# A two-layer streaming trunk on one core: pauses re-ordered, token numbers stored once, and the time-step row in two passes

## The chip, the core and the metric

The kernel runs as one program on one core of a Trainium2 chip. The metric is the time of one execution on the device, in microseconds (us). The engines are called by their names or by those of the profile: TensorE is PE (its weight loads are PEld), VectorE is DVE, ScalarE is ACT, GpSimd is POOL and SyncE is SP. SP issues nearly all DMA transfers.

## What is computed

The input is a sequence of 256 tokens of 1024 channels, in float32. It passes two layers. Each normalises its input, projects it for four token mixers (short gated convolution, state-space mixer, spatial gating, trailing pooling), merges their outputs by sigmoid gates and adds the projected result; then it normalises again and applies a feed-forward part, which is dense in layer 0 and picks 2 of 8 experts for each token in layer 1. A last norm ends it. Cut to what matters here:

```python
for layer in range(2):
    h = rmsnorm(x, norm1_g[layer])
    pa, pb, pc, pd = jnp.split(h @ w_in[layer], [...], -1)
    y_a = short_conv_mixer(...)
    z, xbc, dt_raw = jnp.split(pb, [...], -1)   # dt_raw: 16 heads
    y_b = mamba2_mixer(z, xbc, dt_raw, ...)     # ends with a norm over 4 groups
    y_c, y_d = gmlp_mixer(...), pool_mixer(...)
    gates = sigmoid(h @ w_gate[layer])          # (tokens, 4, 1024)
    merged = sum(gates[:, :, i] * (y @ w_br[layer]) for i, y in enumerate((y_a, y_b, y_c, y_d)))
    x = x + merged @ w_out[layer]
    h2 = rmsnorm(x, norm2_g[layer])
    x = x + (swiglu(h2, ...) if layer == 0 else moe_ffn(h2, ...))   # top 2 of 8 experts
return rmsnorm(x, final_g)

def moe_ffn(x, router_w, wg, wu, wd):
    ...
    for e in range(8):
        out = out + combine[:, e:e + 1] * swiglu(xt, wg[e], wu[e], wd[e])
```

## The kernel before

**Products.** A float32 product of full precision is made from rounded parts. Activations and weights are each split into a high part, rounded to TensorE's faster float32 format, and a low part, the rest. A product is then three matmuls: high by high, high by low and low by high (`product`, L1453). Some small products are made with plain float32 operands; the profile counts each of those as two instructions. `mm` (L1445) issues every matmul, so nearly all of TensorE's time stands on that line.

**Weights.** All weights come as units of 128 x 2048 float32 values (1 MB). SP loads them into a ring of `RING` = 3 slots (7 in the expert stage). ScalarE rounds a unit to its high part (`split`, L416; `split_e`, L448), VectorE subtracts to get the low part (L745, L789), and TensorE uses the unit and raises `unit_used`, which frees the slot. Both engines split `AHEAD` = 2 units ahead of TensorE. A layer's mixers have 54 units: 0 to 23 the input projection, 24 to 41 the gates and output projections of three branches, 42 to 45 the gate of the state-space branch, 46 to 49 its projection, 50 to 53 the output projection. The dense feed-forward has 33 units (11 steps of 3). An expert item has 42 units, in 7 chunks of 6.

**Order.** The engines run their own instruction streams and meet at semaphores. The order of the mixers' smaller work around the units is a list written by hand, `PLAN` (L69): pairs of a stage's name and the number of units that follow. Every engine walks this list. On ScalarE the convolutions, `var`, `spatial`, `pool_out` and `short` are run behind the split of the unit that follows them; every other stage, and on VectorE all of them, is run ahead of it.

**The norms** (`norm_sums`, L1479). ScalarE squares the pairs of channel tiles (L433). GpSimd adds the second and the third pair to the first (`squares_added`, L1326). TensorE sums over the channels with a matrix of ones: four products, of tiles 0, 1, 6 and 7. This is called three times: for the dense part's norm in layer 0, and for layer 1's two norms. The dense part's input rows are `yb_hi`/`yb_lo`, the mixers' are `h_hi`/`h_lo`.

**The time steps.** The weights of the 16 time-step columns are split on their own into `wdt_hi` and `wdt_lo`. TensorE makes a row of 16 x 256 with 24 matmuls (stage `dt_row`), ScalarE copies it, and TensorE transposes it in two halves (stage `dt_in`).

**State-space norm** (stage `y_norm`, the last of `PLAN`). TensorE spreads the groups' sums over the channels, VectorE multiplies by them (L1021) and makes the low part (L748), ScalarE the high part of `yb`. Unit 46 is the first to use them. Stage `short` (L538 on ScalarE) makes the short convolution's rows `y_hi`/`y_lo` in the same way, and `pool_out` those of the pooling.

**Experts.** After the router, every expert's tokens are packed into items of up to 128 rows; with these inputs there are 8 items. Seven of them run in a loop (`body`), the last behind it. An item's units are the gate, up and down weights, chunk by chunk. The rows of a coming item are gathered from DRAM (`rows`) by GpSimd with an indirect DMA, whose row numbers are made thus: VectorE compares the slots with a counting row (`picks`, L1155), TensorE multiplies the result by the token numbers behind chunk 3 (four instructions), and VectorE copies the column to integers (`row_id`). Ahead of the loop, TensorE makes the first item's hidden rows from units 0 to 3 (`up`, L1791), then uses unit 4 and turns the hidden rows for the way down (L1892); VectorE splits units 4, 5 and 6, multiplies the gate (`gated`, L1179) and splits unit 7.

**The end.** The last item's results go to DRAM (`made`), come back in each token's order and are added; the final norm follows. ScalarE scales the rows of one half of the tokens by the norm, VectorE those of the other; each half of the tokens is stored by one transfer.

## Time and profile before

| | |
|---|---|
| time, median of 3 executions | 1858.77 us (1858.38 to 1862.35) |
| the profiled execution | 1860.32 us |
| its span | 1858.5 us |
| TensorE's mean granted clock | 0.997 of full speed |
| TensorE busy | 1838.1 us, 99% of the span, 10331 matmuls |
| VectorE, ScalarE, GpSimd busy | 80%, 64%, 10% |
| DMA, mean over the span | 280 GB/s |

The span runs from the first to the last instruction that the profiler recorded; the rest of an execution's time lies around it. The times of the rows further down are counted from the span's start. A matmul's recorded duration is longer than the distance to the next one, since matmuls are pipelined: those of 512 columns last 0.39 us and start 0.227 apart, those of 256 columns last 0.28 and start 0.12 apart.

### The profile page before, as it was taken

What the parts mean: (1) busy time and instruction counts of PE and PEld (TensorE: products, weight loads), DVE (VectorE), ACT (ScalarE), POOL (GpSimd) and SP (SyncE); (2) the same over time, 40 slices, a digit from 0 to 9 for tenths busy, and PEclk for the clock granted to TensorE, in tenths of its full rate; (3) what the DMA queues carried; (4) which work ended last, traced back from release to release, by engine and by line L of the source; (5) the groups of instructions that cost most, each with busy time, mean ns of one, the idle gap of its engine ahead of it and who ended that gap; (6) DMA issues with size and microseconds to landing.
All of it is one profiled execution on the core that took longest, in us unless ns stands there. A gap on an engine that the chain in (4) does not pass through costs nothing.

```text
span 1858.5 us, 27339 instructions
## 1 busy us (share of the span) xinstructions
PE 1838.1 (99%) x10331; PEld 1595.2 (86%) x10331; DVE 1483.2 (80%) x1308; ACT 1192.8 (64%) x1010; POOL 193.7 (10%) x147
## 2 busy tenths in 40 slices
PE   9999999999999999999999999999999999999997
PEld 8998878999999998779788888888888888888876
DVE  7776677755578866776988988888899898988887
ACT  5655654533346546555767777777777777877775
POOL 1055000000010460000840000000000000000010
PEclk9999999999999999999999999999999999999999
DMA  9454455455454444446799999999999999999994
GB/s 355 173 182 159 160 180 176 165 184 188 174 200 164 154 179 169 172 160 237 303 375 372 385 389 377 367 373 393 384 377 375 369 394 378 373 375 381 385 393 174
DMA packets 74545, 521.27 MB, mean 280 GB/s; under 512 B 8176, under 2 KB 8432, under 8 KB 13680
## 3 DMA queue, kind: packets, MB, share of 16 engines
q1 hardware_dynamic: 71568, 509.34, 72.7%
q0 software_dynamic: 2912, 11.01, 1.6%
q8 instruction: 47, 0.77, 0.2%
q14 instruction: 18, 0.15, 0.0%
HBM read 509.83 MB, written 10.49 MB: 280 GB/s over the span
## 4 chain that ended last, share of the span: by engine, by line
PE 94%; DVE 2%; DMA 2%; ACT 1%; issue 1%; SPq 0%; DVEq 0%; ACTq 0%
PE psum L1445 92%; PE psum L1892 1%; DMA weight_raw<-mix_w 1%; DMA weight_raw<-moe_w 1%; DVE proj L1021 0%; PE psum L1820 0%; DVE yb_lo L748 0%; DVE weight_raw_r L789 0%; DVE yb_lo L755 0%; PE psum L1528 0%; PE psum L1652 0%; DVE proj L771 0%; DVE weight_lo L1035 0%; DVE weight_lo L745 0%; ACT proj L717 0%
## 5 line engine op out<-in xcount | busy, mean ns | idle before, releaser
L745 DVE TENSOR_TENSOR weight_lo<-weight_raw,weight_hi 128x2048 fp32r<-128x2048 f32 x139 | 329.3, 2370 | 151.8 <-ACT weight_hi L416 150.8
L416 ACT ACTIVATE weight_hi<-weight_raw 128x2048 fp32r<-128x2048 f32 x139 | 265.2, 1910 | 144.2 <-PE psum L1445 140.4
L1445 PE MATMUL psum<-weight_lo,y_hi 128*128 128x512 f32 x768 | 304.3, 396 | 0.0
L1445 PE MATMUL psum<-weight_hi,y_hi 128*128 128x512 f32 x768 | 301.2, 392 | 2.4 <-DVE y_lo L748 1.8
L1445 PE MATMUL psum<-weight_hi,y_lo 128*128 128x512 f32 x768 | 299.8, 390 | 0.0
L1445 PE MATMUL psum<-weight_lo,y_lo 128*128 128x512 f32 x672 | 262.5, 391 | 0.0
L1445 PE MATMUL psum<-weight_raw_r,y_hi 128*128 128x512 f32 x576 | 224.9, 390 | 0.0
L1445 PE MATMUL psum<-proj_r,y_hi 128*128 128x512 f32 x576 | 224.4, 390 | 0.0
L1445 PE MATMUL psum<-h_hi,weight_hi 128*128 128x256 f32 x704 | 201.1, 286 | 0.0
L1445 PE MATMUL psum<-h_lo,weight_hi 128*128 128x256 f32 x704 | 199.2, 283 | 0.0
L1445 PE MATMUL psum<-h_hi,weight_lo 128*128 128x256 f32 x704 | 199.2, 283 | 0.0
L789 DVE TENSOR_TENSOR weight_raw_r<-weight_raw,weight_lo 128x2048 fp32r<-128x2048 f32 x72 | 165.0, 2291 | 36.6 <-ACT weight_lo L448 36.1
L789 DVE TENSOR_TENSOR weight_raw_r<-weight_raw,weight_hi 128x2048 fp32r<-128x2048 f32 x72 | 166.1, 2307 | 25.1 <-ACT weight_hi L448 24.6
L448 ACT ACTIVATE weight_hi<-weight_raw 128x2048 fp32r<-128x2048 f32 x72 | 138.2, 1919 | 64.7 <-DMA weight_raw<-moe_w 63.4
L789 DVE TENSOR_TENSOR proj_r<-proj,weight_hi 128x2048 fp32r<-128x2048 f32 x72 | 164.7, 2288 | 13.0 <-ACT weight_hi L448 13.0
L789 DVE TENSOR_TENSOR proj_r<-proj,weight_lo 128x2048 fp32r<-128x2048 f32 x72 | 164.9, 2291 | 11.1 <-ACT weight_lo L448 10.4
L1445 PEld LDWEIGHTS psum<-weight_hi,y_hi 128*128 128x128 f32 x768 | 144.3, 188 | 33.3 <-DVE h_hi L789 2.0
L1445 PEld LDWEIGHTS psum<-weight_hi,y_lo 128*128 128x128 f32 x768 | 144.4, 188 | 30.3
L448 ACT ACTIVATE weight_lo<-weight_raw 128x2048 fp32r<-128x2048 f32 x72 | 138.1, 1919 | 49.8 <-DMA weight_raw<-moe_w 49.6
L1445 PEld LDWEIGHTS psum<-weight_lo,y_hi 128*128 128x128 f32 x768 | 144.5, 188 | 28.5
L448 ACT ACTIVATE weight_hi<-proj 128x2048 fp32r<-128x2048 f32 x72 | 138.6, 1925 | 36.2 <-DMA proj<-moe_w 31.2
L448 ACT ACTIVATE weight_lo<-proj 128x2048 fp32r<-128x2048 f32 x72 | 138.3, 1921 | 27.4 <-DMA proj<-moe_w 26.5
(315 smaller groups left out, 3802.0 us busy)
## 6 DMA issues: line engine op xcount, KB each, us to landing
proj<-moe_w SPq DMA_DIRECT2D x144, 1024.0 KB, 6.9
weight_raw<-moe_w SPq DMA_DIRECT2D x144, 1024.0 KB, 6.8
weight_raw<-mix_w SPq DMA_DIRECT2D x106, 1024.0 KB, 4.8
first_raw<-moe_w SPq DMA_DIRECT2D x48, 1024.0 KB, 7.0
weight_raw<-ff_w SPq DMA_DIRECT2D x33, 1024.0 KB, 4.8
made_rows<-zeros POOLq DMA_DIRECT2D x1, 4096.0 KB, 22.1
made_rows<-pool_tmp SPq DMA_DIRECT2D x8, 512.0 KB, 6.4
weight_raw<-mix_w SPq DMA_DIRECT2D x4, 512.0 KB, 8.4
```

The costliest lines, as they stand in the source:

```text
L416: A(hi[:, slot, :], raw[:, slot, :], ACT.Copy).then_inc(hi_done, 1)
L448: A(hi_e(v), raw_e(v), ACT.Copy).then_inc(hi_done, 1)
L745: V.tensor_tensor(lo[:, slot, :], raw[:, slot, :], hi[:, slot, :].bitcast(f32), ALU.subtract).then_inc(lo_done, 1)
L789: V.tensor_tensor(lo_e(v), raw_e(v), hi_e(v).bitcast(f32), ALU.subtract).then_inc(lo_done, 1)
L1445: return nc.tensor.matmul(o, a, b_, start=start, stop=stop, skip_group_check=True, **k)
L1892: last = nc.tensor.transpose(bank(6)[:, f * P:(f + 1) * P], ff_h[:, f * P:(f + 1) * P], C_("ident"))
```

## The change

- **Norm sums.** GpSimd adds all four pairs of squares into the first and then the two tiles of that pair; TensorE makes one product where it made four.
- **Time-step row.** `wdt_hi` and `wdt_lo` stand side by side in one tile of 32 columns. 16 matmuls replace 24; the row has 32 partitions, and two plain float32 products with `both` (two identity matrices, one over the other) add its halves and turn it.
- **Order of stages.** `y_norm` is run behind the split of the unit that follows, on ScalarE and VectorE; VectorE also runs `short` and the pooling's low part (`pool_low`) so.
- **End of the dense layer.** On VectorE the low part of pair 2 goes ahead of the addition of pair 3.
- **Token numbers.** GpSimd writes the token of every packed row into a DRAM tensor `ids` with four indirect transfers, once. In the loop it loads 128 numbers per item from there. The picks on VectorE, the product on TensorE and the copy of its result go away in the loop; GpSimd waits for `gather_ps` where it waited for `id_done`.
- **First expert units.** `first_up` begins each of the first two units with the products that don't need the rows' low part. VectorE multiplies the first gate ahead of the split of unit 6.
- **Start and end.** SP loads the first half of x ahead of the parameters. The last scaling and the stores are cut in halves of 512 channels.

```diff
+        wdt = sb("wdt", [P, KT, 2 * HEADS], f32r)
+        wdt_hi, wdt_lo = wdt[:, :, 0:HEADS], wdt[:, :, HEADS:]
+        both = sb("both", [2 * HEADS, HEADS])
...
@@ sync
-            sp.dma_start(par[:, :PAR_FIRST], par_in[0, :, :PAR_FIRST]).then_inc(par_loaded, 16)
             for u in range(2):
                 for part in range(2):
                     if u == 0:
                         sp.dma_start(x[:, 4 * part:4 * part + 4, :], x_in[:, 4 * part:4 * part + 4, :]).then_inc(x_loaded[part], 16)
+                    if u == part == 0:
+                        sp.dma_start(par[:, :PAR_FIRST], par_in[0, :, :PAR_FIRST]).then_inc(par_loaded, 16)
...
-            for t in range(TT):
-                sp.wait_ge(*((S["tok_std"], 2 * TT + 1), (S["rstd_done"], 3))[t])
-                sp.dma_start(out[:, t, :], x_gain[:, t, :]).then_inc(stored, 16)
+            for n in range(2):
+                for t in range(TT):
+                    sp.wait_ge(*((S["tok_std"], 2 * TT + 1 + n), (S["rstd_done"], 3 + n))[t])
+                    sp.dma_start(out[:, t, cols(n)], x_gain[:, t, cols(n)]).then_inc(stored, 16)
@@ scalar
-                    behind = name.startswith("conv") or name in ("var", "spatial", "pool_out", "short")
+                    behind = name.startswith("conv") or name in ("var", "spatial", "pool_out", "short", "y_norm")
...
-                for u in range(u, MIX_UNITS):
-                    mixer_unit(layer, u)
+                for m in range(u, MIX_UNITS):
+                    mixer_unit(layer, m, "y_norm" if m == u else None)
@@ vector
                 for name, n in PLAN:
-                    stage(name, layer)
-                    for _ in range(n):
-                        mixer_unit(layer, u)
+                    behind = {"pool_out": "pool_low", "short": "short"}.get(name)
+                    if behind != name and name != "y_norm":
+                        stage(name, layer)
+                    for m in range(n):
+                        mixer_unit(layer, u, behind if m == 0 else None)
                         u += 1
-                for u in range(u, MIX_UNITS):
-                    mixer_unit(layer, u)
+                for m in range(u, MIX_UNITS):
+                    mixer_unit(layer, m, "y_norm" if m == u else None)
...
+                        if q == PAIRS - 1:
+                            low(2, q - 1)
                         added(q)
-                        if q:
+                        if 0 < q < PAIRS - 1:
                             low(2, q - 1)
...
-                    if c == 3 and not final:
-
-                        dve.wait_ge(S["id_ps"], item + 1)
-                        V.tensor_copy(row_id, bank(7)[:, SEQ:SEQ + 1]).then_inc(S["id_done"], 1)
...
-            for v in (4, 5, 6):
-                split_e(v)
+            split_e(4)
+            split_e(5)
             dve.wait_ge(unit_used, RING + MOE_U + 4)
             gated(0, 0)
+            split_e(6)
             split_e(7)
@@ gpsimd
-                for q in (1, 2):
+                for q in range(1, PAIRS):
                     gp.wait_ge(S["sq_done"], PAIRS * n + q + 1)
-                    last = G.tensor_tensor(flat(sq[:, 0:2, :]), flat(sq[:, 0:2, :]), flat(sq[:, 2 * q:2 * q + 2, :]), ALU.add)
-                    if q == 1:
-                        link(last)
-                last.then_inc(S["sq_added"], 1)
+                    link(G.tensor_tensor(flat(sq[:, 0:2, :]), flat(sq[:, 0:2, :]), flat(sq[:, 2 * q:2 * q + 2, :]), ALU.add))
+                G.tensor_tensor(sq[:, 0, :], sq[:, 0, :], sq[:, 1, :], ALU.add).then_inc(S["sq_added"], 1)
...
+            G.tensor_copy(at_id, made_f).then_inc(S["ids_at"], 1)
+            gp.wait_ge(S["ids_at"], 1)
+            gp.wait_ge(made_cleared, 32)
+            for n in range(2):
+                for t in range(TT):
+                    at_ = bass.IndirectOffsetOnAxis(ap=at_id[:, TT * n + t:TT * n + t + 1].bitcast(u32), axis=0)
+                    gp.indirect_dma_start(ids, at_, tok_id[:, t:t + 1], None).then_inc(ids_landed, 16)
...
             with gp.Fori(0, last_item) as item:
-                gp.wait_ge(S["id_done"], item + 1)
+                gp.wait_ge(S["gather_ps"], 2 * item + 2)
+                gp.dma_start(row_id, ids[ds((item + 2) * P, P), :]).then_inc(ids_landed, 16)
+                gp.wait_ge(ids_landed, 16 * (item + 1 + 2 * TT))
@@ tensor
-                for k in (0, 1, KT - 2, KT - 1):
-                    if k == 0:
-                        pe.wait_ge(S["sq_added"], n + 1)
-                    elif k == KT - 2:
-                        pe.wait_ge(S["sq_done"], PAIRS * (n + 1))
-                    last = mm(bank(7)[:, 0:SEQ], C_("ones"), sq[:, k, :], k == 0, k == KT - 1)
-                last.then_inc(S["norm_sum"], 1)
+                pe.wait_ge(S["sq_added"], n + 1)
+                mm(bank(7)[:, 0:SEQ], C_("ones"), sq[:, 0, :], True, True).then_inc(S["norm_sum"], 1)
...
-                        mm(o, wdt_hi[:, k, :], h_hi[:, k, :], k == 0, False)
-                        mm(o, wdt_hi[:, k, :], h_lo[:, k, :], False, False)
-                        last = mm(o, wdt_lo[:, k, :], h_hi[:, k, :], False, k == KT - 1)
+                        mm(o, wdt[:, k, :], h_hi[:, k, :], k == 0, False)
+                        last = mm(o, wdt[:, k, :], h_lo[:, k, :], False, k == KT - 1)
...
-                        last = nc.tensor.transpose(bank(6)[:, SEQ + t * HEADS:SEQ + (t + 1) * HEADS], row[:, t * P:(t + 1) * P],
-                                                   C_("ident")[0:HEADS, 0:HEADS])
+                        last = mm(bank(6)[:, SEQ + t * HEADS:SEQ + (t + 1) * HEADS], row[:, t * P:(t + 1) * P], both[:], True, True)
...
+            def first_up(half):
+
+                split_e_is(half, 0)
+                pe.wait_ge(S["eg_hi_done"], half + 1)
+                for k in range(4):
+                    w, kk = slice(k * CHUNK_F, (k + 1) * CHUNK_F), 4 * half + k
+                    mm(bank(4), xg_hi[:, kk, :], hi_e(half)[:, w], kk == 0, False)
+                    mm(bank(4), xg_hi[:, kk, :], lo_e(half)[:, w], False, False)
+                pe.wait_ge(S["eg_lo_done"], half + 1)
+                for k in range(4):
+                    kk = 4 * half + k
+                    last = mm(bank(4), xg_lo[:, kk, :], hi_e(half)[:, k * CHUNK_F:(k + 1) * CHUNK_F], False, kk == KT - 1)
+                last.then_inc(unit_used, 1)
...
-                    if c == 3 and not final:
-
-                        pe.wait_ge(S["pick_done"], item + 2)
-                        for t in range(TT):
-                            last = mm(bank(7)[:, SEQ:SEQ + 1], pick[:, t, :].bitcast(f32), C_("tok_id", t, 1), t == 0, t == 1)
-                        last.then_inc(S["id_ps"], 1)
...
-            for v in range(4):
-                if v < 2:
-                    pe.wait_ge(S["eg_lo_done"], v + 1)
-                if v == 2:
-                    pe.wait_ge(S["x_tok_done"], 2 * TT)
-                up(bank(4 + v // 2), v, v % 2)
+            first_up(0)
+            first_up(1)
+            pe.wait_ge(S["x_tok_done"], 2 * TT)
+            up(bank(5), 2, 0)
+            up(bank(5), 3, 1)
```

## Rows read from the trace of the kernel before

**Rows 1.** The page, busy time and share of the span of each engine.

```profile
PE 1838.1 (99%) x10331; PEld 1595.2 (86%) x10331; DVE 1483.2 (80%) x1308; ACT 1192.8 (64%) x1010; POOL 193.7 (10%) x147
```

**Rows 2.** Timeline of TensorE, dense layer: start us, us, engine, line, what.

```profile
351.80 1.89 PE L1445 MATMUL psum<-proj,con 128*128 128x256 f32 x8
...
353.34 0.47 PE L1445 MATMUL psum<-yb_hi,weight_hi 128*128 128x256 f32 x1
```

**Rows 3.** Timelines of ScalarE, VectorE and GpSimd, start and end of the dense layer.

```profile
348.07 0.62 ACT L433 ACTIVATE proj<-x 128x512 f32<-128x512 f32 x1
...
351.17 2.28 DVE L745 TENSOR_TENSOR weight_lo<-weight_raw,weight_hi 128x2048 fp32r<-128x2048 f32 x1
...
537.39 2.86 POOL L1330 TENSOR_TENSOR proj<-proj 128x512 f32<-128x512 f32 x2 [191.45 <-ACT proj L433]
```

**Rows 4.** Timelines of TensorE and VectorE, time-step row of both layers.

```profile
36.08 0.28 PE L1445 MATMUL psum<-h_hi,wdt_hi 128*16 128x256 f32 x1 [0.90 <-DVE h_lo L748]
...
562.22 1.48 DVE L748 TENSOR_TENSOR h_lo<-proj,h_hi 128x512 fp32r<-128x512 f32 x2
...
564.58 0.28 PE L1445 MATMUL psum<-h_hi,wdt_hi 128*16 128x256 f32 x1
...
567.39 0.28 PE L1445 MATMUL psum<-h_hi,weight_hi 128*128 128x256 f32 x1
```

**Rows 5.** Chain that ended last, two stretches of one item: start us, us, work.

```profile
1057.39 16.37 PE psum L1445 x72
...
1074.20 16.88 PE psum L1445 x76
```

**Rows 6.** Timelines of TensorE and VectorE, start of the experts.

```profile
898.82 0.48 PE L1445 MATMUL psum<-weight_hi,y_hi 128*128 128x512 f32 x1
...
903.80 0.44 PE L1892 MATMUL psum<-con,proj 128*128 128x128 f32 x2 [1.98 <-DVE proj L1179]
...
895.21 3.54 DVE L789 TENSOR_TENSOR weight_raw_r<-weight_raw,weight_hi 128x2048 fp32r<-128x2048 f32 x1
...
900.87 2.28 DVE L789 TENSOR_TENSOR h_hi<-first_raw,weight_hi 128x2048 fp32r<-128x2048 f32 x1
...
903.07 0.67 DVE L1179 TENSOR_TENSOR proj<-proj,psum 128x512 f32<-128x512 f32 x1
...
910.28 0.68 DVE L748 TENSOR_TENSOR y_lo<-psum,y_hi 128x512 fp32r<-128x512 f32 x1
```

**Rows 7.** Timelines of TensorE and VectorE, end of the dense layer.

```profile
541.18 0.38 PE L1445 MATMUL psum<-yb_hi,weight_hi 128*128 128x256 f32 x1 [1.04 <-DVE yb_lo L755]
...
542.25 2.55 DVE L745 TENSOR_TENSOR weight_lo<-weight_raw,weight_hi 128x2048 fp32r<-128x2048 f32 x1
```

**Rows 8.** Timelines of TensorE and VectorE, SSM norm of layer 0.

```profile
291.51 0.40 PE L1445 MATMUL psum<-weight_hi,h_lo 128*128 128x512 f32 x1
...
293.66 3.22 DVE L1021 SCALAR_TENSOR_TENSOR proj<-proj,par,psum 128x256 f32<-128x256 f32 x8 [2.71 <-PE psum L1445]
...
296.81 2.43 DVE L748 TENSOR_TENSOR yb_lo<-proj,yb_hi 128x1024 fp32r<-128x1024 f32 x2
...
299.39 0.47 PE L1445 MATMUL psum<-weight_hi,yb_hi 128*128 128x512 f32 x1 [0.28 <-DVE yb_lo L748]
```

**Rows 9.** Timelines of ScalarE and TensorE, short convolution of layer 0.

```profile
168.13 1.92 ACT L416 ACTIVATE weight_hi<-weight_raw 128x2048 fp32r<-128x2048 f32 x1 [4.12 <-PE psum L1445]
...
173.31 0.39 PE L1445 MATMUL psum<-weight_hi,y_hi 128*128 128x512 f32 x1
```

**Rows 10.** Stretches: us, busy us (count) by engine, TensorE clock, DMA share, GB/s.

```profile
903.80:907.20 3.40, 3.40 (x17) 2.89 (x18) 3.40 (x2) 2.41 (x2) 3.40 (x2) 1.00 1.01 423
...
1797.20:1800.60 3.40, 1.61 (x9) 1.17 (x8) 3.40 (x3) 2.90 (x2) 0.00 (x0) 1.00 1.02 424
...
1800.60:1804.00 3.40, 3.40 (x10) 2.63 (x9) 3.40 (x3) 2.38 (x2) 0.00 (x0) 0.50 1.00 417
```

**Rows 11.** Timeline of ScalarE, last scaling.

```profile
1852.96 1.15 ACT L727 ACTIVATE proj<-proj,small 128x1024 f32<-128x1024 f32 x1 [0.23 <-DVE small L1309]
```

59 lines of the change are left out of this document (31 added, 28 removed).

## The prediction

> **What bounds the kernel now.** I began with the busy line [rows 1]: TensorE is busy for 1838.1 of 1858.5 us. The other engines have slack, so an edit counts only if it takes instructions off TensorE, or shortens or lengthens one of its few pauses. The longest wait of TensorE is 2.0 us [rows 6], so I read the timelines around each pause and asked of every moved step: when does TensorE need its result, and when will it have it now?
>
> **Terms that take work off TensorE.**
>
> *Norm sums.* Each of three calls issues four products, recorded as eight instructions, from 351.80 to the next matmul at 353.34 [rows 2]: 1.54 us. One product is a quarter, so each call sheds about 1.2 us. In exchange GpSimd adds the last pair of squares and folds the pair, and TensorE waits for that.
> In the dense layer the last squares end at 348.07 + 0.62 = 348.69 [rows 3]. A GpSimd addition of 512 columns takes 1.43 (two in 2.86 [rows 3]), and one of 256 columns half of it. That makes 350.8, or 351.2 with two semaphores, before 351.80. The saving stands: -1.2. If the fold has to stand behind VectorE's next split (351.17, 2.28 us [rows 3]), it ends near 354.2 and the term turns to about +1.2.
> The Trainium skill has a rule here (SBUF — State Buffer, section "SBUF: two separate sides"): VectorE with two SBUF inputs and a GpSimd operation that reads SBUF take an exclusive lock, and the later one waits for the whole instruction. By that rule the fold is either in time or a whole split late, and nothing between.
> In layer 0, TensorE stands before the time-step row until 36.08, waiting 0.90 for h_lo [rows 4], which in the code stands behind ACT's and VectorE's splits of the first weight units, not behind the sums alone. The time saved only lengthens this wait: 0. Putting x ahead of the parameters moves the same bytes ahead of those weights: 0 too.
> In layer 1, the two last pairs of h_lo are finished at 562.22 + 1.48 = 563.70 and TensorE wants them at 564.58 [rows 4]. This chain starts at TensorE's unit before, not at the sums, so only the slack of about 0.8 can be had: -0.8 (from 0 to -1.2).
>
> *Time-step row.* 24 matmuls run from 564.58 to 567.39 [rows 4], 0.117 us each; 8 fewer in each layer is -1.9. The two transposes that follow become plain f32 products, which this kernel records as two instructions each. The nearest price is four such small instructions in 0.51 us [rows 5]: two more per layer, about +0.25, together +0.5 (between 0, if only the streaming counts, and 0.5).
>
> *Token numbers.* Seven of the eight items carry a stretch of 76 matmuls in 16.88 us where the others have 72 in 16.37 [rows 5]. The difference, 0.51 us, is the product with the token numbers, now taken out: 7 x 0.51 = -3.6. 72 matmuls of the stretch take 72 x 0.227 = 16.4, so there is no pause in it that could take this back. GpSimd instead writes the numbers once with four small indirect transfers and reads 128 of them per item before its gather. It waits on its own queue alone, an item ahead of need. I take 0; it would cost only if the rows came later than five such stretches on, 5 x 16.4 = 82 us.
>
> **Terms on pauses.**
>
> *Start of the experts.* The new order lets TensorE start its first expert unit without the low part, under 1 us earlier. But unit 4 then waits: its split runs from 895.21 for 3.54 us, to 898.75, and TensorE uses it at 898.82 already [rows 6]. This half is 0. The second half is real. TensorE stands until 903.80 for the product that VectorE makes at 903.07, behind the split that began at 900.87. With that split moved behind, the product starts at 900.87 and ends at 901.55; TensorE has issued unit 4 at 901.65 (12 matmuls of 0.23 after 898.82), so 2.1 us go. What is late next: VectorE works without a break from 895.21 to 910.96, where the low part of the hidden rows ends [rows 6]. TensorE, 2.1 earlier, would now want it about 0.6 before it is there. Net -1.5 (from -2.1 to -0.8).
>
> *End of the dense layer.* The low part of pair 2 goes ahead of the addition of pair 3. TensorE gets pair 2 at 541.18 [rows 7]; the first of its two instructions still ends with GpSimd's additions at 537.39 + 2.86 = 540.25 [rows 3], so it gains 0.2. But the addition of pair 3 slips by 1.8, and ACT and the low part of pair 3 with it; the weight split queued behind them slips from 542.25 to about 543.4 [rows 7]. TensorE needs this split 36 matmuls of 0.12 us after pair 2, at 545.3. It ends at 545.7, or, if GpSimd's new third addition (1.4 us, woken near 543.1) comes between, at 547.0. So +0.4 or +1.7 (from 0 to 1.7): I take +1.0.
>
> *The SSM norm moves behind a split.* This is the largest term, and it is a loss. VectorE has stood for 2.71 us when the spread sums come at 293.66; then it normalises and makes both low parts, until 299.24. TensorE starts on them at 299.39, after a pause of 0.28 [rows 8]. Now the split of unit 47 comes first. It can't fill the idle 2.71: its high part goes into a slot that is free only when unit 44 is used, and TensorE's last matmul of that unit ends at 291.51 + 0.40 = 291.91 [rows 8]. ACT needs 1.92 [rows 9], so VectorE could split from 293.95 to 296.2 at the earliest. The norm then starts 2.5 later and TensorE with it, in both layers: 2 x 2.5 = +5.1. The bounds are 0 (split hidden) and 2 x 2.9.
>
> *The short convolution's low part moves behind a split.* ACT finishes the high part of that split at 168.13 + 1.92 = 170.05. VectorE then splits to 172.3 and makes the low part (1.21, half of two in 2.43 [rows 8]) to 173.5, and TensorE wants it at 173.31 [rows 9]. With a restart +0.4 per layer, +0.8 (from 0 to 1.2). The pool's low part moves behind a split in the same way, but several units ahead of its first use: 0.
>
> *Output in halves.* The last scaling takes 1.15 [rows 11]. Its halves let stores start about 0.5 earlier, and the fourth store costs one more issue. I take -0.3 (from 0 to -0.6).
>
> **Sum.** -1.2 - 0.8 - 1.9 + 0.5 - 3.6 - 1.5 + 1.0 + 5.1 + 0.8 - 0.3 = -1.9 us.
>
> **The clock.** Near the end TensorE paused and was busy for 1.61 of 3.40 us; in the next 3.40 its granted clock was 0.50, that is 1.2 instead of 2.4 GHz [rows 10]. Half speed for 3.40 us costs at most 1.7; I take 1.6. The pause of 1.98 before 903.80 [rows 6] drew none: 1.00 in the 3.40 us behind it [rows 10]. The new pause before the SSM product is 0.28 + 2.5 = 2.8, twice: I expect a spell after one of the two, +1.6, which makes -0.3.
>
> The Trainium skill speaks against this change here (TensorE: Matmul & The Clock Gate, section "HAM oscillation — how this bites in real kernels"): where the engine waits for its input between bursts, each wait can throttle it and the next burst starts at the low clock. By that rule both pauses draw a spell and the sum would be +1.3; the trace agrees with its one spell and disagrees with its 1.98 us pause.
>
> The profiled execution took 1860.3 us, 1.8 of it around its span of 1858.5, and is 1.5 over the median of 1858.8. The sum is made against that span; the 1.8 around it stay, so the difference is carried over to the median: 1858.8 - 0.3 = **1858.5**.
>
> **Rivals.**
> - *Forecast* (0.45): both y_norm pauses grow, with one or two slow spells: -0.3 to +1.3, 1858.5 to 1860.1.
> - *No spell* (0.17): the pause before 903.80 speaks for it. -1.9, 1856.9.
> - *The split hides* (0.15): the norm is not late, because VectorE gets the high part before its idle 2.7 us. Against it: ACT can't write the slot before unit 44 is used. -1.9 - 5.1 = -7.0, 1851.8.
> - *The item time does not fall* (0.08): if the arrival of weights held the loop, the 3.6 would be lost: +1.7, 1860.5 with no spell, 1862.1 with one. Against it: a stretch is as long as its matmuls make it [rows 5].
> - *Slower* (0.15): the clock, after the two long pauses, stays at half for most of the unit that follows. At half clock each us costs 0.5, so it decides once the two spells together last more than 2 x (3.7 + 1.9) = 11.2 us; at 6.6 us each they cost 6.6 and it is -1.9 + 6.6 = +4.7, 1863.5. Against it: the one spell seen had ended after 3.4 us with TensorE busy.
>
> **Numbers.** 0.2% is 3.7 us, about what a measurement here can tell. Faster: the hidden split 0.15 and 0.05 for other terms better than taken. Slower: 0.15 plus 0.02 of the fourth case with two spells. Same: the rest, 0.63. The range goes from 1853.0 to 1863.0; outside lie the third case and part of the last, together about 0.2. The terms' own bounds (-0.8 to +0.6 at the experts and the dense layer's end, 2.4 at the fold) fit in it.
>
> **What will show it.** In the profile after: TensorE before its first product with yb_hi waits about 2.8 us for VectorE's yb_lo in both layers, with the granted clock at 0.50 behind at least one; before the first product with y_hi and the short convolution's rows a new wait of 0.3; the norm sums x2 instead of x8; the wait at the expert start gone from 2.0 to nearly 0, with a new short one for y_lo some 7 us on; the stretches of 76 matmuls gone from the seven items, each item 0.5 shorter. The prediction is wrong if yb_lo is not late, if the fold misses its moment, or if an item does not shorten.

## The result, and the profile after

The changed kernel takes 1866.85 us (median of 6, 1863.32 to 1868.91) beside 1859.37 for the kernel before (6, 1858.36 to 1862.35). The ratio is 1.0038, with a 95% interval of 1.0028 to 1.0048: about 7 us slower. The prediction was 1858.5 with a range up to 1863.0. The time lies above the range, in the case "slower", which had been given 0.17.

The profiled execution of the changed kernel took 1865.16 us, with a span of 1863.2; that is 4.7 over the span of before. The page and the waits of TensorE show the kind of thing that happened:

```profile
PE 1832.1 (98%) x10273; PEld 1588.1 (85%) x10273; DVE 1472.8 (79%) x1289; ACT 1188.8 (64%) x1011; POOL 247.2 (13%) x167
```

```profile
PE psum L1458 <- DVE yb_lo L754: 5.5, 2, 2.8
PE psum L1458 <- DVE y_lo L754: 4.3, 3, 2.7
PE psum L1458 <- POOL proj L1334: 2.1, 1, 2.1
PE psum L1458 <- DVE h_lo L754: 2.1, 2, 1.7
...
PE psum L1458 <- DVE weight_lo L751: 1.2, 1, 1.2
PE psum L1458 <- DVE weight_raw_r L795: 1.1, 2, 0.6
```

(Columns: who waited for whom, us in total, times, the longest.) TensorE is busy for 6.0 us less than in [rows 1], so the work did leave it. It stands longer: for yb_lo as forecast; for two things that the sum did not hold, a GpSimd addition (L1334, the fold) and y_lo 2.7 us long; and for a weight split (L751), which the sum held in its +1.0 for the end of the dense layer.

The reader can place each gain and loss by comparing the start of one and the same instruction of TensorE in both traces. The rows of after that answer to those of before:

```profile
36.45 0.28 PE L1458 MATMUL psum<-h_hi,wdt 128*32 128x256 f32 x1 [1.69 <-DVE h_lo L754]
...
173.39 0.47 PE L1458 MATMUL psum<-weight_hi,y_hi 128*128 128x512 f32 x1
...
302.05 0.47 PE L1458 MATMUL psum<-weight_hi,yb_hi 128*128 128x512 f32 x1 [2.75 <-DVE yb_lo L754]
...
356.75 0.70 PE L1458 MATMUL psum<-proj,con 128*128 128x256 f32 x2 [2.11 <-POOL proj L1334]
357.10 0.47 PE L1458 MATMUL psum<-yb_hi,weight_hi 128*128 128x256 f32 x1
...
544.75 0.38 PE L1458 MATMUL psum<-yb_hi,weight_hi 128*128 128x256 f32 x1 [0.85 <-DVE yb_lo L761]
...
550.52 0.38 PE L1458 MATMUL psum<-yb_hi,weight_hi 128*128 128x256 f32 x1 [1.20 <-DVE weight_lo L751]
...
568.86 0.28 PE L1458 MATMUL psum<-h_hi,wdt 128*32 128x256 f32 x1 [0.40 <-DVE h_lo L754]
...
570.72 0.28 PE L1458 MATMUL psum<-h_hi,weight_hi 128*128 128x256 f32 x1
...
834.44 0.47 PE L1458 MATMUL psum<-weight_hi,yb_hi 128*128 128x512 f32 x1 [2.76 <-DVE yb_lo L754]
...
908.09 0.60 PE L1906 MATMUL psum<-con,proj 128*128 128x128 f32 x4
```

Against [rows 4, 9, 8, 2, 7] the changed kernel is late by 0.37 (36.08), 0.08 (173.31), 2.66 (299.39), 3.76 (353.34), 3.57 (541.18), 4.28 (564.58) and 3.33 (567.39). The first product with yb_hi in layer 1 started at 827.91 before; now it is 6.53 late. The product behind the first gate [rows 6] is late by 4.29 (903.80) and waits for nothing any more. The differences between neighbours are the terms: the SSM norm 2.5 in each layer, the dense layer's fold +1.1 where -1.2 was forecast, and so on.

The last part is read from the chain of waits. Before, chunks of the first item follow each other without a break from 904.46. After (short pieces left out):

```profile
926.52 16.37 PE psum L1458 x72
943.33 16.37 PE psum L1458 x72
960.13 8.22 PE psum L1458 x36
968.52 13.37 DMA weight_raw<-moe_w
982.04 1.77 issue
984.30 1.93 ACT weight_lo L453
986.31 2.16 issue
988.46 0.69 DVE y_lo L754
989.27 10.09 PE psum L1458 x36
```

In the middle of the first item the chain leaves TensorE and stands for 13.37 us on a transfer of weights. The 36 matmuls behind it take 10.09 where 36 others take 8.22: for the 3.4 us from 990.1 the granted clock is 0.50. Nothing like it stands in the chain of before at this place, and the forecast had nothing there.

### The profile page after: what moved, and what is told of

Its sections match the earlier page's. It is cut to its first block, busy times and chain, and to the rows that moved or that the text cites. A ratio compares the mean times of both kernels' runs of the same rounds, so it can differ in the third digit from the quotient of the medians.

```text
span 1863.2 us, 27227 instructions
## 1 busy us (share of the span) xinstructions
PE 1832.1 (98%) x10273; PEld 1588.1 (85%) x10273; DVE 1472.8 (79%) x1289; ACT 1188.8 (64%) x1011; POOL 247.2 (13%) x167
## 4 chain that ended last, share of the span: by engine, by line
PE 89%; DVE 5%; DMA 2%; issue 2%; ACT 1%; POOL 0%; SPq 0%; DVEq 0%; ACTq 0%; POOLq 0%
PE psum L1458 87%; DMA weight_raw<-moe_w 1%; PE psum L1906 1%; DMA weight_raw<-mix_w 1%; DVE weight_lo L751 1%; DVE weight_raw_r L795 1%; DVE proj_r L795 1%; ACT weight_hi L421 1%; DVE proj L777 0%; DVE yb_lo L761 0%; DVE proj L1030 0%; PE psum L1840 0%; DVE yb_lo L754 0%; ACT weight_lo L453 0%; DVE h_lo L754 0%
## 5 line engine op out<-in xcount | busy, mean ns | idle before, releaser
L751 DVE TENSOR_TENSOR weight_lo<-weight_raw,weight_hi 128x2048 fp32r<-128x2048 f32 x139 | 322.9, 2324 | 173.6 <-ACT weight_hi L421 172.6
```

The source lines that it names most:

```text
L751: V.tensor_tensor(lo[:, slot, :], raw[:, slot, :], hi[:, slot, :].bitcast(f32), ALU.subtract).then_inc(lo_done, 1)
```

## The experiments

Seventeen runs were made, in five groups; the kernels of one group ran on the same chip and share the runs of the kernel before. Each is compared with that by its ratio; 0.001 is 1.9 us.

**The changed kernel again**, as the base of the first group.

> The changed kernel once more, beside the others of this call. Theory A (five places lose, the largest a weight shortage in the first expert item, which varies from execution to execution): 1863 to 1869 us, and its profile has the same two pauses of 2.8 us before the first product with yb_hi, and a shortage of weights behind the four scattered stores of token numbers. Theory B (the shortage was an accident of one profile): no pause of TensorE over 1 us in the first expert item this time.

1865.35 us, ratio 1.0036 (1.0022 to 1.0050). The same places showed: pauses of 2.9 us beyond the pitch (the distance of two starts, less the 0.227 or 0.12 us that it has without a pause) before both first products with yb_hi, 2.3 at the fold, 2.8 in the first item at 986.88. This time a half-clock spell lay behind the norm of layer 0 and none in the first item. Theory A stands.

**The SSM norm**, put back in the changed kernel, and put alone into the kernel before.

```diff
-... name in ("var", "spatial", "pool_out", "short", "y_norm")
+... name in ("var", "spatial", "pool_out", "short")
...
-                    mixer_unit(layer, m, "y_norm" if m == u else None)
+                    mixer_unit(layer, m)
...
-                    if behind != name and name != "y_norm":
+                    if behind != name:
```

> The changed kernel with the SSM norm run ahead of the split again, on ScalarE and VectorE. Theory A: the two pauses of 2.75 us before yb_hi go back to 0.28, nothing behind them takes the difference, and the time falls by 4.9 us against the changed kernel. Rival: the time lost there is absorbed by the waits that follow (fold, end of the dense layer), and less than 2 us are won.

1860.03 us, ratio 0.9998 (0.9989 to 1.0007): 5.3 us less than the changed kernel by the medians, where 4.9 was expected. The pauses are 0.43 and 0.44 beyond the pitch again.

> The kernel before, with only the SSM norm moved behind the split on ScalarE and VectorE. Theory A: two pauses of 2.75 us before yb_hi instead of 0.28, +4.9 us, and in some executions a half-clock spell behind one of them (+1.6): 1865 to 1867 us, 0.27% to 0.35% over the kernel before. Rival: +2 us or less, because what follows takes it up.

(The edit is the same one the other way round, in the kernel before.) 1867.72 us, ratio 1.0038 (1.0025 to 1.0052), about 7 us: more than the 4.9 of the two pauses. The profiled execution, the slowest of the six (1871.10 us), shows what the rest is made of:

```profile
302.60:306.00 3.40, 3.40 (x9) 2.62 (x10) 0.76 (x1) 2.60 (x3) 0.00 (x0) 0.50 0.02 5
306.00:309.40 3.40, 3.40 (x11) 2.67 (x10) 1.53 (x1) 0.00 (x0) 0.00 (x0) 0.62 0.27 41
```

The clock column is the third from the end. Behind the first pause it is 0.50 for 3.4 us and partly for as long again; a second spell lay behind the other pause, and one each at 547 and 915 us. Over the eight profiles in which the norm stands behind the split there are sixteen such pauses, all of 2.9 us beyond the pitch, and nine were followed by a half-clock spell. It differs between executions of the same kernel (none after either pause in the profile of after, one in its second run). A spell of 3.4 us costs 1.7 us; the one in these two rows lasted 6.8.

**The token numbers**, undone in the changed kernel.

```diff
-                    gp.indirect_dma_start(ids, at_, tok_id[:, t:t + 1], None).then_inc(ids_landed, 16)
...
+                    if c == 3 and not final:
+                        pe.wait_ge(S["pick_done"], item + 2)
+                        for t in range(TT):
+                            last = mm(bank(7)[:, SEQ:SEQ + 1], pick[:, t, :].bitcast(f32), C_("tok_id", t, 1), t == 0, t == 1)
```

> The changed kernel with the token numbers made by a product in every item again, no scattered stores. Theory A (the four scattered stores of 4-byte numbers hold up the weight transfers, which costs the first item 4.0 us of pauses and 1.6 us of half clock): against the changed kernel -5.6 and +3.6 for the seven products, so about -2, or more where its median lies above its profile. Theory B (the first item runs short of weights because TensorE reaches it with less lead, whatever is stored): the pauses stay, the seven products cost 3.6, and the time rises by 3 to 4 us.

1862.70 us, ratio 1.0015 (1.0006 to 1.0023). The time falls although 3.6 us of products came back, and the longest pause in the first item is 0.50. Theory B falls. In this profile the fold was in time as well, of which more below, which is worth some 2.3 us. So the 2.7 us by the medians are not all the stores', and the stores cost between 4.0 and 6.3 us (2.7 + 3.6, with or without the 2.3; an estimate).

**The scattered stores alone**, in the kernel before; run twice. Nothing reads what they store.

```diff
+            for n in range(2):
+                for t in range(TT):
+                    at_ = bass.IndirectOffsetOnAxis(ap=at_id[:, TT * n + t:TT * n + t + 1].bitcast(u32), axis=0)
+                    gp.indirect_dma_start(ids, at_, tok_id[:, t:t + 1], None).then_inc(made_cleared, 16)
+            gp.wait_ge(made_cleared, 32 + 16 * 2 * TT)
```

> The kernel before, with only the four scattered stores of token numbers added behind the tables on GpSimd (nothing reads them; the products stay), and GpSimd waiting for them ahead of its loop. Theory A: the transfer rate falls to under 200 GB/s for about 5 us behind the stores, and TensorE pauses in the first item as in the changed kernel: 3 to 7 us slower than before. Theory B: no pause, the time of before.

1861.45 us, ratio 1.0010 (1.0002 to 1.0019). The profiled execution, the slowest of the eleven, had pauses of 1.4 and 1.7 us in the first item. The direction is right, the price less than expected.

> The kernel before with the four scattered stores alone, a second time, as the base of the two kernels beside it. As the first time: the transfer rate under 200 GB/s for 5 to 10 us behind the stores, pauses of 1.4 to 4 us in the first item, 1 to 4 us slower than before.

1860.57 us, ratio 1.0002 (0.9994 to 1.0011); one pause of 0.54 us. That is less than the 1 to 4 us expected. By the two intervals the stores cost the kernel before between nothing and 3.5 us. Part of why the changed kernel pays more may be that it no longer pauses ahead of the first item, when the weights got ahead of TensorE; that is argued and not shown.

**Every scattered store twice**, in the changed kernel.

```diff
                     gp.indirect_dma_start(ids, at_, tok_id[:, t:t + 1], None).then_inc(ids_landed, 16)
+                    gp.indirect_dma_start(ids2, at_, tok_id[:, t:t + 1], None).then_inc(ids_landed, 16)
```

> The changed kernel with each of the four scattered stores made twice (the second set goes to another tensor that nothing reads). Theory A (the stores take DMA time from the weights): the low stretch of the transfer rate is twice as long and the pauses in the first item grow from 3 or 4 us to 7 or more; the time rises by 3 to 6 us. Rival (GpSimd's waiting or TensorE's earlier start makes the shortage): the time is that of the changed kernel.

1871.81 us, ratio 1.0060 (1.0047 to 1.0074), by the ratios 4 to 5 us over the changed kernel. TensorE's waits in the first item, then the stretches behind the stores, of the changed kernel and of this one:

```profile
PE psum L1459 <- DVE y_lo L754: 5.1, 1, 5.1
PE psum L1459 <- DVE weight_raw_r L795: 3.0, 1, 3.0
```

```profile
955.00:960.00 5.00, 5.00 (x26) 4.17 (x25) 4.84 (x3) 3.27 (x3) 4.18 (x4) 1.00 1.01 393
960.00:965.00 5.00, 5.00 (x24) 4.11 (x23) 4.04 (x3) 3.93 (x5) 4.39 (x3) 1.00 1.33 375
965.00:970.00 5.00, 5.00 (x24) 4.13 (x23) 3.54 (x3) 1.92 (x2) 4.36 (x4) 1.00 0.61 136
970.00:975.00 5.00, 5.00 (x24) 4.14 (x23) 2.89 (x2) 1.77 (x1) 0.00 (x0) 1.00 1.07 289
975.00:980.00 5.00, 4.71 (x23) 3.56 (x21) 2.29 (x1) 2.67 (x2) 0.63 (x1) 1.00 0.94 241
```

```profile
965.00:970.00 5.00, 5.00 (x23) 4.14 (x23) 3.25 (x3) 2.52 (x2) 4.39 (x3) 1.00 0.77 116
970.00:975.00 5.00, 5.00 (x23) 4.13 (x22) 2.89 (x2) 2.16 (x2) 4.37 (x4) 1.00 1.24 308
975.00:980.00 5.00, 5.00 (x25) 4.14 (x24) 2.29 (x1) 0.06 (x1) 2.67 (x3) 1.00 0.75 70
```

The last column is GB/s. In the changed kernel the stores are issued from 955.7 to 964.4 and the rate goes from 393 to 136. In finer slices (0.575 us) it lies under 200 GB/s for 4.0 us from 964.5 and for some 4 us, with a break, from 973.7. With twice as many stores it does so for 4.6 us and then for 6.9, so the second hole, 70 here, is the longer one. TensorE still works (its column is full) on weights that were ahead, and stands 15 to 22 us after the first hole began. That is why the wait stands at y_lo or at a weight split and not at a DMA.

**What in the stores does it?** Their four bytes, or their index? Both edits are against the kernel with the scattered stores alone.

```diff
-                    gp.indirect_dma_start(ids, at_, tok_id[:, t:t + 1], None).then_inc(made_cleared, 16)
+                    gp.dma_start(ids[(TT * n + t) * P:(TT * n + t + 1) * P, :], tok_id[:, t:t + 1]).then_inc(made_cleared, 16)
```

> The kernel before with four stores of 128 x 4 bytes to neighbouring rows (no index), in the place of the four scattered ones; nothing reads them. If the smallness of the stored pieces holds up the weights: the same dip and the same pauses as with the scattered ones. If the index (the indirect form or the scattered addresses) does: no dip below 300 GB/s for over 1 us, and the time of before.

1864.32 us, ratio 1.0028 (1.0017 to 1.0039), with a wait of 2.4 us in the first item. Without an index, and 4 bytes each: the loss is there.

```diff
-    ids = nc.dram_tensor("row_tokens", ((MAX_ITEMS + 1) * P, 1), ...
+    ids = nc.dram_tensor("row_tokens", ((MAX_ITEMS + 1) * P, 128), ...
-                    gp.indirect_dma_start(ids, at_, tok_id[:, t:t + 1], None)...
+                    gp.indirect_dma_start(ids, at_, zeros[:, 0:128].bitcast(i32), None)...
```

> The kernel before with four scattered stores by the same index, but of 512-byte rows (zeros; nothing reads them), in the place of the 4-byte ones. If the smallness does it: 256 KB more to move, 0.7 us at 380 GB/s, and no dip below 250 GB/s; the time of before. If the index does it: the dip and the pauses stay.

1860.14 us, ratio 1.0000 (0.9992 to 1.0009). With the index and 512 bytes a piece, 128 times the bytes: no loss. By the times this kernel differs from that with the plain 4-byte stores, but not from those with the scattered ones (1.0010 and 1.0002), whose intervals overlap with its own. One line of the DMA view separates all three, GB/s in 40 slices of 949 to 972 us: the plain 4-byte stores, the scattered 4-byte ones (second run) and the scattered 512-byte ones:

```profile
GB/s 356 385 356 413 401 300 357 243 157 29 114 142 128 142 128 157 157 114 128 242 385 427 399 399 399 456 427 413 413 427 413 427 442 456 427 413 413 413 427 427
```

```profile
GB/s 342 257 427 442 456 300 413 442 328 242 157 86 43 114 86 57 342 427 456 428 414 385 414 399 356 43 43 71 57 43 214 427 442 328 385 442 442 442 456 427
```

```profile
GB/s 228 242 356 399 442 349 363 413 413 420 428 435 399 456 413 442 413 399 456 427 413 399 427 456 385 385 356 399 328 271 370 413 442 442 356 370 413 399 370 356
```

For 11 slices of 0.575 us, 6.3 us, the plain 4-byte stores, 2 KB in all, leave the weights some 130 GB/s, a third of their rate. The same holes stand in all eleven profiles with 4-byte stores: behind the stores the rate stays under 200 GB/s for at least 2.3 us at a stretch. In the eight without them, two of these with 512-byte stores, it does so for no more than 1.2 us between 945 and 990. The size is the cause. The Trainium skill (DMA: Bandwidth & Descriptors, section "Specifications") says that transfers under 512 bytes are done as read-modify-write and don't reach the line rate. The traces agree that 4 bytes do harm and 512 do not; no size between was run, and they show nothing of the mechanism inside.

**The norm sums.** Undone, and with the fold alone taken out.

```diff
-                for q in range(1, PAIRS):
+                for q in (1, 2):
...
-                mm(bank(7)[:, 0:SEQ], C_("ones"), sq[:, 0, :], True, True).then_inc(S["norm_sum"], 1)
+                for k in (0, 1, KT - 2, KT - 1):
...
+                    last = mm(bank(7)[:, 0:SEQ], C_("ones"), sq[:, k, :], k == 0, k == KT - 1)
```

> The changed kernel with the norm sums as before (GpSimd adds two pairs, four products on TensorE). Theory A (GpSimd's fold of 256 columns and its third addition share a lock with VectorE's split; the fold loses it by 0.15 us in most executions): the pause of 2.3 us in the dense layer goes, for 1.2 us more of products; the pause of 1.4 us near the end of the dense layer shrinks to 0.3; in layer 1 1.2 us of products come back. About -1.5 us against the changed kernel. Rival (the products saved outweigh the waits): +2 us or more.

1863.57 us, ratio 1.0019 (1.0010 to 1.0028), by the ratios 3 to 4 us under the changed kernel where 1.5 was expected. No pause at the fold and none of 1.36 near the end of the dense layer; the pause in the first item was 1.7 us this time, so not all of the gain need be the sums'.

```diff
-                G.tensor_tensor(sq[:, 0, :], sq[:, 0, :], sq[:, 1, :], ALU.add).then_inc(S["sq_added"], 1)
+                last.then_inc(S["sq_added"], 1)
...
-                mm(bank(7)[:, 0:SEQ], C_("ones"), sq[:, 0, :], True, True).then_inc(S["norm_sum"], 1)
+                for k in (0, 1):
+                    last = mm(bank(7)[:, 0:SEQ], C_("ones"), sq[:, k, :], k == 0, k == 1)
```

> The changed kernel without the fold: GpSimd adds the three pairs, TensorE makes two products. Theory A: the third addition still ends before TensorE asks in the dense layer, so the pause of 2.3 us goes and the second product costs 0.43: about -2 us there, and at most 0.4 of it is given back in layer 1. The pause of 1.4 us near the end of the dense layer stays, since the third addition stays. Rival: the wait is for the additions themselves, and the pause stays.

1862.99 us, ratio 1.0013 (1.0004 to 1.0022), by the ratios 4 to 5 us under the changed kernel for the 2 expected; the rest is not explained. The pause at the fold is gone, that of 1.36 stays, as theory A had it. The fold itself is best seen by laying the changed kernel beside the one with the token numbers undone, where it was in time:

```profile
350.74 0.62 ACT L438 ACTIVATE proj<-x 128x512 f32<-128x512 f32 x1
...
351.87 1.30 POOL L1333 TENSOR_TENSOR proj<-proj 128x512 f32<-128x512 f32 x1 [3.26 <-ACT proj L438]
353.25 3.45 POOL L1334 TENSOR_TENSOR proj<-proj 128x256 f32<-128x256 f32 x1
...
353.85 2.28 DVE L751 TENSOR_TENSOR weight_lo<-weight_raw,weight_hi 128x2048 fp32r<-128x2048 f32 x1
```

```profile
353.70 0.74 POOL L1346 TENSOR_TENSOR proj<-proj 128x256 f32<-128x256 f32 x1
...
354.56 2.27 DVE L750 TENSOR_TENSOR weight_lo<-weight_raw,weight_hi 128x2048 fp32r<-128x2048 f32 x1
```

With 0.86 us ahead of VectorE's split, the fold takes 0.74. With 0.60 ahead it takes 3.45 and ends 0.57 us behind the split; four further profiles show the same lead and the same 3.45 (the changed kernel's second run, and those with the SSM norm put back, the stores doubled and the dense layer's old end). But the lead alone does not decide it. In the last of these, the next experiment below, the fold of layer 1 starts 0.05 ahead of a split and takes 0.74, and it is the split that gets longer (2.84 for 2.28):

```profile
552.84 0.74 POOL L1332 TENSOR_TENSOR proj<-proj 128x256 f32<-128x256 f32 x1
...
552.89 2.84 DVE L751 TENSOR_TENSOR weight_lo<-weight_raw,weight_hi 128x2048 fp32r<-128x2048 f32 x1 [1.28 <-ACT weight_hi L421]
```

**The end of the dense layer**, in its old order.

```diff
-                        if q == PAIRS - 1:
-                            low(2, q - 1)
                         added(q)
-                        if 0 < q < PAIRS - 1:
+                        if q:
                             low(2, q - 1)
```

> The changed kernel with the end of the dense layer in its old order (addition of pair 3 ahead of the low part of pair 2). Theory A (the late addition pushes the weight split, whose end TensorE then awaits for 1.36 us): that pause goes, 1.2 us less than the changed kernel. Rival (GpSimd's third addition, which stays, makes the split late): the pause stays at 1 us or more.

1864.20 us, ratio 1.0032 (1.0022 to 1.0042), against 1.0036 and 1.0038 for the changed kernel: the intervals overlap, so the time alone decides nothing. The trace does: the pause of 1.36 us is gone, though the third addition stayed. Both the new order and the third addition are needed to make it, since undoing either took it away. In the changed kernel the two meet: the addition runs from 546.90 for 1.41 us, and VectorE's split from 547.07 takes 3.39 instead of 2.28.

**What is left when the losing parts are taken out.** The norm and the short convolution's low part ahead of the split, the dense layer's old end, two products for a norm sum, token numbers by products:

> What is left when the losing parts are taken out: the changed kernel with the SSM norm and the short convolution's low part ahead of the split, the dense layer's end in its old order, token numbers by products, and two products for a norm sum. From the profile of the kernel with products for the token numbers: span 1860.1, less 4.9 for the norm, 0.6 for the short convolution, 1.6 for its half-clock spell, plus 0.6 for the second products: span 1853.6, time 1855.4, 4 to 5 us under the kernel before. Rival: what is kept (16 matmuls instead of 24, the order at the experts' start) is eaten by waits, and the time is that of the kernel before.

1854.12 us, ratio 0.9964 (0.9950 to 0.9977), by the ratio 6.7 us under the kernel before where 4 to 5 were expected, and a second time:

> The best version with products for the token numbers, a second time, beside the other: 1854 us, 0.3% to 0.4% under the kernel before.

1853.00 us, ratio 0.9970 (0.9959 to 0.9981). The rival, no gain, falls. Two kernels next to it (of the first edit, the lines that `first_up` replaced are left out):

```diff
-            split_e(4)
-            split_e(5)
+            for v in (4, 5, 6):
+                split_e(v)
             dve.wait_ge(unit_used, RING + MOE_U + 4)
             gated(0, 0)
-            split_e(6)
...
-            first_up(0)
-            first_up(1)
```

> The best version so far with the experts' start as before (units 4, 5, 6 split ahead of the first gate, first units with the low part awaited). Theory A: the pause of 2.0 us before the hidden rows are turned comes back, the two new ones of 0.8 go: 1.2 us slower than the best version. Rival: no difference.

1855.78 us, ratio 0.9979 (0.9970 to 0.9988). The interval overlaps with both of the best version, so the times show no difference for sure. In the profiles TensorE reaches the pause before the last item 1.2 us later with the old order; in the first profile of the best version that pause was itself 1.2 longer, and both spans are 1852.3. The order at the experts' start gains its 1.2 us up to there; that the whole time keeps it is likely and not shown.

The other keeps the numbers as the changed kernel stores them:

> The best version so far with the stored token numbers instead of the products. Theory A (the seven products saved, 3.6 us, are worth less than the shortage that the scattered stores make): 1 to 4 us slower than the best version, 1855 to 1858 us, with pauses of 3 us or more in the first expert item. Rival (with more lead in front of the first item the shortage doesn't reach TensorE): 3.6 us faster than the best version, about 1850.5.

1855.70 us, ratio 0.9976 (0.9968 to 0.9985), with a pause of 3.2 us and a half-clock spell of 6.8 us in the first item. With the 3.6 us of the products saved and nothing lost, the ratio would be 0.9945 to 0.9951. That lies outside the interval. So the 4-byte stores eat at least about all that they save, here too; that the kernel is slower than the one with products is not clear of the noise.

**The numbers stored once, but 512 bytes wide.**

```diff
+            wide = zeros[:, 0:TT * 128].bitcast(i32).rearrange("p (t c) -> p t c", t=TT)
+            G.tensor_copy(wide, tiles(C_("tok_id"), 1).broadcast_to([P, TT, 128]))
...
-                    gp.indirect_dma_start(ids, at_, tok_id[:, t:t + 1], None).then_inc(ids_landed, 16)
+                    gp.indirect_dma_start(ids, at_, wide[:, t, :], None).then_inc(ids_landed, 16)
...
-                gp.dma_start(row_id, ids[ds((item + 2) * P, P), :]).then_inc(ids_landed, 16)
+                gp.dma_start(zeros[:, 256:384].bitcast(i32), ids[ds((item + 2) * P, P), :]).then_inc(ids_landed, 16)
```

> The best version with the token numbers stored once, but as rows of 512 bytes (128 copies of the number) that are scattered and read back whole. If only the 4-byte size of the stores did the harm: no dip behind the stores, no pause over 1 us in the first item, and the 3.6 us of the seven products are saved: 1850 to 1851.5 us, 0.5% under the kernel before. If the 64 KB that each item reads now, or the larger clearing at the start, cost as much: the time of the best version.

1850.87 us, ratio 0.9949 (0.9936 to 0.9963), by the ratio 9.5 us under the kernel before (8.3 by the medians), and the lowest time of all. Against the same kernel with 4-byte rows (0.9976) the intervals are apart, by 5 us at the middle: the width turns a loss into a gain. The rows are read back 512 bytes wide as well, which was not tried by itself. Against the best version with products (0.9970) the intervals still touch; in the profiles TensorE is 3.2 us ahead at the last item. The chain runs through the place where it broke off:

```profile
933.67 16.37 PE psum L1460 x72
950.04 0.44 PE psum L1910 x4
950.48 16.37 PE psum L1460 x72
966.85 0.44 PE psum L1910 x4
967.28 16.37 PE psum L1460 x72
```

## Why the prediction was wrong

**The token numbers: the step that failed.** The prediction said of the stores and loads: "It waits on its own queue alone, an item ahead of need. I take 0". It asked only who waits for these transfers and not what they do to the others. The -3.6 of the products was right; the stores cost 4.0 us of pauses beyond the pitch, in three pieces, and 1.8 of a half-clock spell in the profile of after, and 0.5 to 4.5 us of pauses in the nine other profiles with single stores of 4 bytes. The rival "the item time does not fall" had the supply of weights in view, but as a steady limit in all items; it is one hole in the first.

**The norm sums: right mechanism, mis-sized term.** In the dense layer -1.2 was forecast and +1.1 came. The prediction had priced this case itself ("the term turns to about +1.2") and left it out, because it put the fold's end at 351.2 against a split at 351.17 and asked only whether TensorE's moment, 351.80, was met. In the trace the third addition started 0.51 us behind the last squares (351.36 to 351.87), so the fold came 0.6 ahead of the split and needed 0.74. By the rule of the Trainium skill that was cited (SBUF — State Buffer, "SBUF: two separate sides") a fold that comes after the split is a whole split late. The trace agrees on the price (3.45 us for 0.74). It does not agree on who waits: the fold's recorded start lay 0.60 us ahead of the split's, and with 0.05 ahead in layer 1 of another run the split waited. What decides it stays open. In layer 1 the products saved 1.2; 0.56 beyond the pitch of it came back as a wait for h_lo, so -0.6 for -0.8. In layer 0 the time was taken as 0, which held as far as the sums go. A word on the text above: the three calls are for layer 0's first norm, the dense norm and layer 1's first norm; the expert norm has its own products.

**The SSM norm: right.** +5.1 was forecast for two pauses, and 2.47 + 2.48 = 4.95 measured in the pauses, 2.58 + 2.56 = 5.1 by the starts of the rows around them. VectorE's rows after are those of the working, the split first, then the norm and the low parts until 301.91:

```profile
294.13 2.29 DVE L751 TENSOR_TENSOR weight_lo<-weight_raw,weight_hi 128x2048 fp32r<-128x2048 f32 x1 [2.99 <-ACT weight_hi L421]
296.34 3.21 DVE L1030 SCALAR_TENSOR_TENSOR proj<-proj,par,psum 128x256 f32<-128x256 f32 x8
299.48 2.43 DVE L754 TENSOR_TENSOR yb_lo<-proj,yb_hi 128x1024 fp32r<-128x1024 f32 x2
```

**The clock: right in kind.** One spell behind the two pauses was forecast; nine in sixteen is 1.1 for two, so +1.9 instead of +1.6 on average. The profile of after had none there and one in the first item, and it lost the one of before behind the last item's pause, which is 0.88 us now and was 1.78. By the citation of the Trainium skill (TensorE: Matmul & The Clock Gate, "HAM oscillation — how this bites in real kernels") the prediction had both pauses draw one: 9 of 16 do. That section tells of waits longer than these, so the rule was stretched. The rival "slower", two spells of 6.6 us each behind the two pauses, was not seen in any profile (one single spell of 6.8 was); the slower result came from another cause, so the 0.17 given to "slower" was right by luck as far as it was right.

**The rest.** Time-step row: 567.39 - 564.58 = 2.81 became 570.72 - 568.86 = 1.86, -0.95 in layer 1 and -0.9 in layer 0 (38.87 - 36.08 against 38.34 - 36.45), as forecast; the two turning products cost 0.3 a layer for 0.25. In layer 0 the row starts 0.37 late, because h_lo comes later (the wait is 1.69 for 0.90): ScalarE got the third weight unit at 24.52 instead of 24.14. The end of that wait lies between 35.6 and 37.5 us in the profiles. The end of the dense layer: +1.0 forecast, and -0.2 at pair 2 with +1.36 at the split makes +1.2. (The 0.2 came with the norm sums, not with the order: the wait at pair 2 is 0.84 with the old order and the new sums, 1.04 with the new order and the old sums.) The start of the experts: from 6.53 late at 834.44 to 5.25 late at 926.52 (921.27 before), -1.3 for -1.5, with the short new waits for y_lo that were expected. Short convolution: 0.3 in each layer, for 0.4. Output in halves: from the last product with weights (1845.76 and 1850.75) to the end 12.7 us before and 12.5 after, -0.3.

**The sum.** For the profiled execution, by the starts of the same products in both traces, with the late h_lo counted to the time-step row of layer 0: -0.2 - 0.6 (time-step rows) + 0.6 (short) + 5.1 (norm) + 1.1 - 0.6 (norm sums) + 1.2 (dense end) - 1.3 (experts' start) - 3.6 + 4.0 + 1.8 (token numbers and stores) - 0.9 - 1.6 (last item's pause and its spell) - 0.3 + 0.4 (a wait in a middle item that went, a new one in the last) - 0.3 (stores of the output) = +4.8 from rounded terms, against 4.7 measured. The two large misses are 2.3 at the fold and 5.8 at the stores. The median of after lies some 2.6 us further above that of before than the profile's difference. The three slowest of its six executions have a lower mean clock (0.994 to 0.996) than the profiled one (0.997), which would fit more half-clock spells, but no trace of them splits it up.

## What to carry to other kernels

When a transfer is added, ask what it does to the transfers beside it, not only who waits for it; 512 stored numbers of 4 bytes took two thirds of the weights' rate away for 6 us, and the same stores 512 bytes wide left no such hole. When GpSimd must get a short operation in ahead of VectorE's long ones, count the start-up behind its semaphore (0.5 us here) and don't rely on a lead of less than its duration, or take the operation out. A pause of TensorE costs itself and, by chance, a half-clock spell as well, so a change whose pauses sum to nothing is not neutral.

## What was not expected of the hardware

- Four stores of 128 x 4 bytes to DRAM, scattered or not, brought the transfers of the core from about 400 GB/s to some 130 for 6 us (plain), or to between 40 and 160 in two holes of 2 to 5 us (scattered). The DMA engines were shown as busy for much of it: share 0.61 to 0.77 in the three stretches of 5 us above that moved 70 to 136 GB/s. TensorE's pause came 10 us (plain) to 20 us later.
- Whether a pause of 2.9 us is followed by the half clock differs between executions: both, one or none of the two pauses. Shorter ones can be followed by it as well: in the kernel with the SSM norm moved alone, one of 1.2 us at 547.12 was; in the kernel before the same pause was not.
- A GpSimd addition of 256 columns took 3.45 us with a lead of 0.60 us on VectorE's split, 0.74 us with a lead of 0.86, and 0.74 us again with a lead of 0.05.
